# Two-block transformer on one core: in the mixers' second phase, the recurrent branch's steps are put in front of the forgetting-attention step that they are dealt with

## The chip, the cores and the metric

The kernel runs on one core of one Trainium2 chip. The metric is the device time of one execution in microseconds. Engines are named as in the profile: PE (TensorE), DVE (VectorE), ACT (ScalarE), POOL (GpSimd), SP (SyncE).

## The reference, cut to what matters

The program is a first block of two layers and a second block with gated linear attention and a mixture of experts. The change is inside the four mixers of the first block's layers; the rest is the same text in both kernels.

```
for l in range(DEPTH):                                   # DEPTH = 2
    pa, pb, pc, pd = _split(h @ w_in[l], GROUP_COLS)
    ya = _rwkv7_mixer(pa, ...)                           # the recurrent branch
    yb = _diff_attn_mixer(pb, ...)                       # differential attention
    yc = _spatial_gating_mixer(pc, ...)                  # gating
    yd = _forgetting_attn_mixer(pd, ...)                 # forgetting attention
    x = x + g1 * (concatenate([ya, yb, yc, yd]) @ w_out[l])
```

Forgetting attention, for each of 4 heads and each of 4 blocks of 128 queries:

```
s = (einsum('bhqd,bhkd->bhqk', qb, k) * scale + (Fq[..., :, None] - F[..., None, :]))
pr = softmax(where(mask, s, NEG_INF), axis=-1)
out = einsum('bhqk,bhkd->bhqd', pr, v)
```

The recurrent branch is a scan over 512 tokens with a 64 x 64 state per head. The kernel cuts it into chunks of 64 tokens, works out each chunk's inner products and its triangular inverse first, and then scans over the 8 chunks.

## The kernel before, in words

All tensors are fp32, features on the 128 partitions, the 512 tokens along the free dimension. Each layer has three parts: the input projection, `mixers`, and a part with the output projection and the feed-forward network. The weights of the projections pass through a ring of four slots in SBUF.

`mixers` (L1820) runs four streams on each engine: 0 is attention (`attention_stream`: gating, preparation, forgetting attention, then differential attention), 1 is the recurrent branch (`rwkv_stream`), 2 a small modulation stream, 3 the opening of the output projection. Each stream is a generator for each engine, and a `yield` ends a step. `run` (L587) takes a list of stream numbers, the plan, and for each entry lets that stream issue one step on the engine. PE, ACT and DVE get the same plan. It sets the order of the instructions in each engine's queue and nothing else: the streams wait for each other's results by semaphores, an engine executes its queue in order, and so an instruction that waits holds back all that stand behind it. POOL has a short list of its own, and SP issues its DMAs without the plan.

`alternate(first, second)` (L1472) gives `first` zeros with `second` ones spread behind them.

The phase that the change touches deals 17 forgetting steps (stream 0) and 30 recurrent steps (stream 1, second half of the features, `prepare(1)` and `intra(1)`). The names used below:

- **F(u)**, u = 0 to 15, is a step of forgetting attention for unit u, a head and a block of 128 queries. Unit u has (u mod 4) + 1 key blocks of 128, so its tiles are 128 to 512 wide. On PE, F(u) issues the scores of unit u+2 (L778, which wait for the exponentials of unit u), the value sums of unit u-1 (L789), and the transposes of unit u (L806, called **T(u)**), which wait for DVE's scaling of unit u. On DVE, F(u) is the mask and the maximum of unit u+1 (L994, L996), then the reciprocal and the scaling of unit u (L1005, L1008). On ACT it is the exponential of unit u+1 (L898) and the copy of T(u) out of PSUM (L909). F(0) also holds units 0 and 1. F(16) is the last value sum and four tiny DVE operations (L1011 to L1016).
- **p0 to p3** are the four steps of `prepare(1)`. p0: on DVE six operations of 128x512 (L1364 to L1370), on ACT four copies (L1288). p1: on ACT the square (L1291) and three exponentials (L1293 to L1295); on PE transposes (L1143) and the sum of the squares (L1149, which waits for the square); on DVE a clamp of that sum (L1373). p2: on ACT L1298, L1300 and four copies; on DVE L1376 to L1382. p3: on PE one sum (L1153); on DVE L1385 to L1394.
- **m0 to m12** are the 13 micro-steps of `intra(1)`, each in two steps, g0 and g1, for four chunks each. Each has 4, 8 or 12 matmuls or transposes on PE (L1177 to L1212) whose results ACT, DVE or both take. m(k+1) of a group waits for what m(k) of the same group left. m0 starts after L1394 and is followed on DVE by four operations (L1414 to L1417) per group.

A matmul of fp32 operands appears in the trace as two instructions, so "x16" stands for 8 of the code's.

The recurrent steps that `prepare` issues on PE, and its square on ACT, read:

```
eng.wait_ge(s["kk_sq"], of("kk_sq", 1))
eng.matmul(PS(3), c.const("bo64"), ss, start=True, stop=True).then_inc(s["kk_ss"], 1)
...
on(ss, kk, ACT.Square).then_inc(s["kk_sq"], 1)
```

Of the kernel before, what the change touches and what calls it, by code (L numbers as in the profile page):

```python
# [586 lines left out]
def run(engine, streams, plan):  # L587

    programs = [s[engine]() for s in streams]
    for i in plan:  # L590
        next(programs[i])
    for p in programs:
        for _ in p:
            raise ValueError("the plan ends before the stream")
# [877 lines left out]
def alternate(first, second):  # L1472

    plan, done = [], 0
    for i in range(first):
        plan.append(0)
        upto = (i + 1) * second // first
        plan += [1] * (upto - done)
        done = upto
    return plan  # L1480
# [237 lines left out]
def modulation_stream(c, mod, turned_after):  # L1718

    nc = c.nc  # L1720

    def pe():
        for j in range(mod.ada.count):
            mod.sum_quarter(j)
        yield
        nc.tensor.wait_ge(*turned_after)
        mod.turn(nc.tensor)
        yield

    def act():  # L1730
        for j in range(mod.ada.count):
            mod.copy_quarter(nc.scalar, j)
        yield
        yield

    def dve():
        yield
        mod.add_bias(nc.vector)
        yield

    return dict(pe=pe, act=act, dve=dve, sp=lambda: mod.spread(nc.sync), steps=2)
# [78 lines left out]
def mixers(c, sums, w_out, ahead):  # L1820

    nc = c.nc
    mod = ModRows(c, "mod", sums, lambda j: c.vt[:, j // 2, j % 2 * S:(j % 2 + 1) * S], lambda j: c.ps[:, A_BANK + j, :],
                  c.ps[:, A_BANK + 3, :])
    att = attention_stream(c, mod, nc)
    modulation = modulation_stream(c, mod, att["roped"])
    rw = rwkv_stream(c, att, w_out, nc)
    a, b = att["steps"], rw["steps"]
    plan = [1] * b["shift"] + [2] + [0] * a["first"] + [1, 1, 1, 1]
    plan += alternate(a["gating"] + a["prepare"], b["intra"]) + [2]  # L1830
    plan += alternate(a["forget"], b["prepare"] + b["intra"])
    last = alternate(a["diff"], b["scan"])
    at = len(last) - 1 - last[::-1].index(0)
    plan += last[:at] + [3] + last[at:] + [3, 1, 0, 1, 3, 0, 3, 1, 3]
    opened = open_out_stream(c, att, rw, w_out)
    streams = [att, rw, modulation, opened]
    with nc.Block() as block:
        @block.sync
        def _(sp):
            sp.wait_ge(c.tables_in, 32)  # L1840
            att["sp"]()
            modulation["sp"]()
            rw["sp"]()

        @block.gpsimd
        def _(pool):
            c.sweep(pool, [*ahead.loaded, ahead.high, ahead.low])
            run("pool", streams[:2], [0, 1, 0, 1, 0, 1, 0])

        @block.tensor  # L1850
        def _(pe):
            run("pe", streams, plan)

        @block.scalar
        def _(act):
            run("act", streams, plan)

        @block.vector
        def _(dve):
            run("dve", streams, plan)  # L1860
# [379 lines left out]
def block_one_layer(c, layer, ahead, w_out, swept, held):  # L2240
    nc = c.nc
    c.layer = layer
    with c.unswept() as early:
# [3 lines left out]
        with c.stages():  # L2247
            mixers(c, mod_sums, w_out, ahead)
# [1686 lines left out]
```

## Time and profile before

| what | before |
|---|---|
| median of 3 runs | 2516.99 us (2516.23 to 2519.7) |
| the profiled execution, its own time | 2517.74 us |
| its span in the profile | 2516.0 us |
| PE busy | 2267.9 us (90%) |
| DVE busy | 1588.7 us (63%) |
| ACT busy | 1076.0 us (43%) |
| mean granted TensorE clock | 0.967 |
| the changed phase, layer 1 | 269 to 366 us |
| the same phase, layer 2 | 1112 to 1209 us |

How to read it: the times are of one execution, and the span is from the profile's first to its last instruction; 1.7 us of the execution's time lie outside it. The "PEclk" of a stretch is the clock that TensorE was granted as a share of 2.4 GHz: 1.00 is 2.4 GHz and 0.50 is 1.2 GHz; a value between means that it changed in the stretch. A row of the timeline gives the start, the time that the group took, the engine, the line, and in brackets how long the engine sat idle before it and what ended that.

### The profile page before, as it was taken

To read this page: it belongs to the slowest core of one execution; us is meant where nothing else is said; L and a number is where in the kernel's file an instruction comes from. 1 tells how busy PE (TensorE), PEld (TensorE's weight loads), DVE (VectorE), ACT (ScalarE), POOL (GpSimd) and SP (SyncE) were. 2 spreads that over 40 slices of the span, in tenths; PEclk is the share of its full clock that TensorE was granted. 3 is DMA by queue.
4 is the path that set the end of the run, shared out by engine and by line. 5 is a ranking of instruction groups with operands and counts; after the bars stand their busy time and mean duration, and the time that the engine had idled before them with its cause. 6 is when DMAs were issued, how large, how long until landed. Compare 5 with 4: busy or idle time off the path is not lost. (4 is left out here: it accounts for less than half of the span.)

```text
span 2516.0 us, 31937 instructions
## 1 busy us (share of the span) xinstructions
PE 2267.9 (90%) x11349; PEld 1812.1 (72%) x11349; DVE 1588.7 (63%) x2284; ACT 1076.0 (43%) x1628; POOL 123.4 (5%) x201
## 2 busy tenths in 40 slices
PE   4998689899999989877889999999999888799995
PEld 3776566678888877666667888787877676588884
DVE  6655656565557665665665555774543774699996
ACT  3343234443343225342343333413333443588884
POOL 0001110000000000110000000000000000011112
PEclk9999899999999999999999999999999999799997
DMA  7650000222225355200012223354634001699996
GB/s 292 210 184 12 1 34 1 76 84 92 94 79 204 128 166 201 77 1 1 35 43 82 94 92 103 137 172 168 218 109 147 22 1 44 265 410 411 412 412 226
DMA packets 95433, 348.32 MB, mean 138 GB/s; under 512 B 12360, under 2 KB 14520, under 8 KB 95056
## 3 DMA queue, kind: packets, MB, share of 16 engines
q1 hardware_dynamic: 88688, 323.67, 36.1%
q0 software_dynamic: 3888, 14.16, 1.5%
q10 hardware_dynamic: 2736, 8.92, 0.9%
q8 instruction: 71, 1.16, 0.2%
q14 instruction: 50, 0.41, 0.1%
HBM read 333.55 MB, written 21.54 MB: 141 GB/s over the span
## 5 line engine op out<-in xcount | busy, mean ns | idle before, releaser
L500 PE MATMUL ps<-a_hi,w_hi 128*128 128x512 f32 x1344 | 545.1, 406 | 28.5 <-DVE h_lo L406 17.8
L502 PE MATMUL ps<-a_hi,w_lo 128*128 128x512 f32 x1344 | 537.2, 400 | 0.0
L501 PE MATMUL ps<-h_lo,w_hi 128*128 128x512 f32 x1280 | 507.8, 397 | 0.0
L464 DVE TENSOR_TENSOR w_lo<-ring,w_hi 128x1024 fp32r<-128x1024 f32 x178 | 218.1, 1226 | 376.1 <-ACT w_hi L459 375.6
L459 ACT ACTIVATE w_hi<-ring 128x1024 fp32r<-128x1024 f32 x178 | 187.9, 1058 | 510.4 <-PE ps L502 505.0
L500 PEld LDWEIGHTS ps<-a_hi,w_hi 128*128 128x128 f32 x1344 | 255.3, 190 | 98.3 <-issue 26.4
L502 PEld LDWEIGHTS ps<-a_hi,w_lo 128*128 128x128 f32 x1344 | 255.4, 190 | 63.0
L501 PEld LDWEIGHTS ps<-h_lo,w_hi 128*128 128x128 f32 x1280 | 243.1, 190 | 60.8 <-issue 2.9
L3392 DVE TENSOR_TENSOR moe_w_lo<-p,moe_w_hi 128x1024 fp32r<-128x1024 f32 x204 | 240.2, 1219 | 17.8 <-ACT moe_w_hi L3489 12.0
L3489 ACT ACTIVATE moe_w_hi<-p 128x1024 fp32r<-128x1024 f32 x204 | 216.2, 1062 | 68.2 <-PE ps L3432 50.6
L2139 PE MATMUL ps<-p_lo,down_hi 128*128 128x512 f32 x352 | 137.8, 392 | 0.0
L3430 PE MATMUL ps<-moe_w_hi,moe_x_hi 128*128 128x512 f32 x272 | 109.0, 401 | 4.9 <-DVE moe_w_lo L3392 2.9
L3432 PE MATMUL ps<-moe_w_lo,moe_x_hi 128*128 128x512 f32 x272 | 107.5, 395 | 0.0
L3431 PE MATMUL ps<-moe_w_hi,moe_x_lo 128*128 128x512 f32 x272 | 107.3, 395 | 0.0
L2056 ACT ACTIVATE down_hi<-down_raw 128x1408 fp32r<-128x1408 f32 x32 | 44.1, 1379 | 144.7 <-PE ps L2140 144.7
L501 PE MATMUL ps<-y_lo,w_hi 128*128 128x512 f32 x192 | 76.5, 398 | 0.0
L2139 PEld LDWEIGHTS ps<-p_lo,down_hi 128*128 128x128 f32 x352 | 66.1, 188 | 14.4
L291 DVE SCALAR_TENSOR_TENSOR y<-vt,cond,y 128x1024 f32<-128x1024 f32 x56 | 70.7, 1279 | 5.9 <-DMA vt<-in_ada 5.9
L2060 DVE TENSOR_TENSOR down_lo<-down_raw,down_hi 128x1408 fp32r<-128x1408 f32 x32 | 52.0, 1624 | 33.7 <-ACT down_hi L2056 33.4
L1991 DVE SCALAR_TENSOR_TENSOR y<-ps,cols,y 128x510 f32<-128x510 f32 x88 | 65.9, 748 | 11.0 <-DVE y L1988 0.5
L1961 ACT ACTIVATE y<-ps,cols 128x512 f32<-128x512 f32 x88 | 67.2, 764 | 9.4 <-PE ps L502 9.4
L1988 DVE SCALAR_TENSOR_TENSOR y<-ps,cols,y 128x511 f32<-128x511 f32 x88 | 65.6, 745 | 4.6 <-ACT y L1961 4.6
(645 smaller groups left out, 4196.0 us busy)
## 6 DMA issues: line engine op xcount, KB each, us to landing
ring<-in_ffn_up SPq DMA_DIRECT2D x88, 512.0 KB, 3.4
ring<-in_w_in SPq DMA_DIRECT2D x72, 512.0 KB, 5.2
p<-in_moe_gate SPq DMA_DIRECT2D x68, 512.0 KB, 7.1
p<-in_moe_up SPq DMA_DIRECT2D x68, 512.0 KB, 6.8
p<-in_moe_down SPq DMA_DIRECT2D x68, 512.0 KB, 8.4
vt<-in_ada SPq DMA_DIRECT2D x64, 512.0 KB, 4.0
p<-in_ada SPq DMA_DIRECT2D x48, 512.0 KB, 5.5
down_raw<-in_ffn_down SPq DMA_DIRECT2D x32, 704.0 KB, 5.2
```

Of the source, the lines that this page charges most:

```text
L291: ins = nc.vector.scalar_tensor_tensor(out, self.piece[b], factor, out, ALU.mult, ALU.add)
L459: self.c.nc.scalar.activation(self.c.w_hi[:, s % 2, :], self.c.slot(s), ACT.Copy).then_inc(self.high, 1)
L464: self.c.nc.vector.tensor_tensor(self.c.w_lo[:, s % 2, :], self.c.slot(s), self.c.w_hi[:, s % 2, :].bitcast(F32), ALU.subtract).then_inc(s ...
L500: nc.tensor.matmul(bank, c.w_hi[:, s % 2, at], hi(kt), start=(kt == self.order[0]), stop=False)
L501: nc.tensor.matmul(bank, c.w_hi[:, s % 2, at], lo(kt), start=False, stop=False)
L502: return nc.tensor.matmul(bank, c.w_lo[:, s % 2, at], hi(kt), start=False, stop=(kt == self.order[-1]))
L2139: nc.tensor.matmul(bank, down.w_hi[n % 2][:, at], c.p_lo[:, kt, :], start=False, stop=False)
L3392: ops.tensor_tensor(m.w_lo[:, n % 4, :], m.raw[n], m.w_hi[:, n % 4, :].bitcast(F32), ALU.subtract).then_inc(low[n], 1)
L3430: nc.tensor.matmul(bank, x[0], w_hi, start=start, stop=False)
L3431: nc.tensor.matmul(bank, x[1], w_hi, start=False, stop=False)
L3432: return nc.tensor.matmul(bank, x[0], w_lo, start=False, stop=stop)
L3489: nc.scalar.activation(m.w_hi[:, n % 4, :], m.raw[n], ACT.Copy).then_inc(high[n], 1)
```

## The change

One line of `mixers`. Before, each forgetting step is followed by its one or two recurrent steps; now F(0) comes first, and each of the other 16 forgetting steps follows its one or two recurrent steps.

```diff
@@ -1828,7 +1828,7 @@
     a, b = att["steps"], rw["steps"]
     plan = [1] * b["shift"] + [2] + [0] * a["first"] + [1, 1, 1, 1]
     plan += alternate(a["gating"] + a["prepare"], b["intra"]) + [2]
-    plan += alternate(a["forget"], b["prepare"] + b["intra"])
+    plan += [0] + [1 - i for i in alternate(b["prepare"] + b["intra"], a["forget"] - 1)]
     last = alternate(a["diff"], b["scan"])
     at = len(last) - 1 - last[::-1].index(0)
     plan += last[:at] + [3] + last[at:] + [3, 1, 0, 1, 3, 0, 3, 1, 3]
```

The two plans of the phase, 47 entries each:

```
before 01011011011010110110110101101101101011011011011
after  01101101101101101101101011011011011011011011010
```

The recurrent steps that stand ahead of F(0), F(1), ... F(16):

```
before  0 1 3 5 7  8 10 12 14 15 17 19 21 22 24 26 28
after   0 2 4 6 8 10 12 14 15 17 19 21 23 25 27 29 30
```

No instruction is added or removed, and the queues of POOL and SP are the same.

ACT, the start of the phase, from p0's copies (L1288) on. Before:

```order
L1288 ACTIVATE p<-p 64x4x64 x4
L898 ACTIVATE ring,small<-ps,small 128x384
L909 ACTIVATE ring<-ps 128x256
L1291 ACTIVATE ring<-ring 128x512
L1293 ACTIVATE vt<-ring 128x512
L1294 ACTIVATE ring<-ring 128x512
L1295 ACTIVATE ring<-ring 128x512
L1298 ACTIVATE ring<-ring 128x512
```

and after:

```order
L1288 ACTIVATE p<-p 64x4x64 x4
L1291 ACTIVATE ring<-ring 128x512
L1293 ACTIVATE vt<-ring 128x512
L1294 ACTIVATE ring<-ring 128x512
L1295 ACTIVATE ring<-ring 128x512
L898 ACTIVATE ring,small<-ps,small 128x384
L909 ACTIVATE ring<-ps 128x256
L1298 ACTIVATE ring<-ring 128x512
```

The square and the exponentials of p1 no longer stand behind the exponential of F(1) and the copy of T(1).

PE, the same place, from T(0) on. Before:

```order
L806 MATMUL ps<-k,ring 128x128
L778 MATMUL ps<-w2b,vt 128x512
L789 MATMUL ps<-ring,vt 64x128
L806 MATMUL ps<-k,ring 128x128 x2
L1143 MATMUL ps<-k,p 128x128 x8
L1149 MATMUL ps<-ring,k 128x512
L778 MATMUL ps<-ring,vt 128x128
L789 MATMUL ps<-ring,vt 64x128 x2
L806 MATMUL ps<-k,ring 128x128 x3
L1153 MATMUL ps<-p,k 128x512
L1177 MATMUL ps<-h,p 128x128
```

and after:

```order
L806 MATMUL ps<-k,ring 128x128
L1143 MATMUL ps<-k,p 128x128 x8
L1149 MATMUL ps<-ring,k 128x512
L778 MATMUL ps<-w2b,vt 128x512
L789 MATMUL ps<-ring,vt 64x128
L806 MATMUL ps<-k,ring 128x128 x2
L1153 MATMUL ps<-p,k 128x512
L778 MATMUL ps<-ring,vt 128x128
L789 MATMUL ps<-ring,vt 64x128 x2
L806 MATMUL ps<-k,ring 128x128 x3
L1177 MATMUL ps<-h,p 128x128
```

The transposes and the sum of p1 stand ahead of F(1), and p3's sum ahead of F(2), which is now the last thing before m0.

DVE, around the end of p3 and m0. Before:

```order
L1391 TENSOR_TENSOR h<-ring 64x8x64 x2
L1394 TENSOR_TENSOR p<-ps,p 128x512
L1414 TENSOR_TENSOR ring<-ps,k 128x512
L1415 TENSOR_TENSOR ring<-ps,k 128x512
L1416 TENSOR_TENSOR y<-ring,k 128x512
L1417 TENSOR_TENSOR ring<-ps,k 128x512
L994 TENSOR_TENSOR ps<-ps,k 128x128
L996 TENSOR_REDUCE small<-ps 128x1
L1005 RECIPROCAL small<-small 128x1
L1008 TENSOR_SCALAR ring<-ring,small 128x512
```

and after:

```order
L1391 TENSOR_TENSOR h<-ring 64x8x64 x2
L1394 TENSOR_TENSOR p<-ps,p 128x512
L994 TENSOR_TENSOR ps<-ps,k 128x128
L996 TENSOR_REDUCE small<-ps 128x1
L1005 RECIPROCAL small<-small 128x1
L1008 TENSOR_SCALAR ring<-ring,small 128x384
L1414 TENSOR_TENSOR ring<-ps,k 128x512
L1415 TENSOR_TENSOR ring<-ps,k 128x512
L1416 TENSOR_TENSOR y<-ring,k 128x512
L1417 TENSOR_TENSOR ring<-ps,k 128x512
```

F(2) now stands between p3 and m0; behind it both groups of m0 come ahead of F(3), where before only the first did.

## Rows read from the trace of the kernel before

**Rows 1.** Windows, core 0: stretch and length, each engine's busy us, PEclk, DMA share, GB/s

```profile
269.00:294.00 25.00, 11.84 (x42) 6.88 (x41) 19.06 (x35) 10.59 (x26) 6.00 (x9) 0.71 0.00 1
...
1113.50:1138.00 24.50, 11.35 (x38) 6.84 (x38) 18.21 (x33) 10.00 (x25) 5.27 (x8) 0.68 0.00 1
```

**Rows 2.** Waits of PE, 269 to 366 us: us in total, times, longest

```profile
PE ps L806 <- DVE ring L1008: 22.6, 15, 4.5
```

**Rows 3.** Timeline of DVE, p0 to p3: start, us, line, tiles, idle before

```profile
277.90 0.30 DVE L994 TENSOR_TENSOR ps<-ps,k 128x128 f32<-128x128 f32 x1
...
283.21 0.69 DVE L1373 TENSOR_SCALAR ring<-ps 128x512 f32<-128x512 f32 x1 [3.96 <-PE ps L1149]
...
286.83 0.30 DVE L994 TENSOR_TENSOR ps<-ps,k 128x128 f32<-128x128 f32 x1
...
287.96 0.42 DVE L1008 TENSOR_SCALAR ring<-ring,small 128x384 f32<-128x384 f32 x1
288.30 0.68 DVE L1385 TENSOR_TENSOR ring<-ring 128x512 f32<-128x512 f32 x1
...
292.62 0.69 DVE L1394 TENSOR_TENSOR p<-ps,p 128x512 f32<-128x512 f32 x1
```

**Rows 4.** Timeline of ACT, p0's copies and p1's square

```profile
274.04 1.72 ACT L1288 ACTIVATE p<-p 64x256 f32<-64x256 f32 x4
...
280.31 0.62 ACT L1291 ACTIVATE ring<-ring 128x512 f32<-128x512 f32 x1
```

**Rows 5.** Timeline of PE, from T(1) to T(3)

```profile
279.31 0.69 PE L806 MATMUL ps<-k,ring 128*128 128x128 f32 x2 [4.26 <-DVE ring L1008]
279.79 1.91 PE L1143 MATMUL ps<-k,p 128*128 128x128 f32 x8
281.49 1.68 PE L1149 MATMUL ps<-ring,k 128*128 128x512 f32 x2
...
288.44 0.90 PE L806 MATMUL ps<-k,ring 128*128 128x128 f32 x3 [4.46 <-DVE ring L1008]
289.13 1.92 PE L1153 MATMUL ps<-p,k 128*128 128x512 f32 x2
293.46 0.77 PE L1177 MATMUL ps<-h,p 128*128 128x128 f32 x2 [2.42 <-DVE p L1394]
...
301.41 0.66 PE L806 MATMUL ps<-k,ring 128*128 128x128 f32 x4 [3.27 <-DVE ring L1008]
```

**Rows 6.** Timelines of PE and DVE, m0 of the first half, no F between

```profile
212.34 6.48 PE L1177 MATMUL ps<-h 128*128 128x128 f32 x32 [4.46 <-DVE p L1394]
...
216.19 0.69 DVE L1414 TENSOR_TENSOR ring<-ps,k 128x512 f32<-128x512 f32 x1 [3.99 <-PE ps L1177]
...
218.97 0.68 DVE L1414 TENSOR_TENSOR ring<-ps,k 128x512 f32<-128x512 f32 x1
```

**Rows 7.** Windows, short stretches: columns as in rows 1

```profile
212.00:215.00 3.00, 2.66 (x12) 2.69 (x13) 0.20 (x1) 0.00 (x0) 0.00 (x0) 0.50 0.00 0
...
286.00:288.00 2.00, 0.00 (x0) 0.00 (x0) 1.86 (x6) 0.86 (x3) 0.00 (x0) 0.55 0.00 0
...
296.00:298.00 2.00, 2.00 (x14) 1.57 (x13) 0.63 (x1) 0.00 (x0) 0.00 (x0) 0.89 0.00 0
298.00:300.00 2.00, 0.14 (x2) 0.00 (x0) 1.90 (x4) 0.00 (x0) 0.00 (x0) 1.00 0.02 4
```

**Rows 8.** Timeline of PE: T(5), both groups of m2, T(6), T(15)

```profile
315.17 0.44 PE L806 MATMUL ps<-k,ring 128*128 128x128 f32 x2 [1.73 <-DVE ring L1008]
315.44 3.74 PE L1177 MATMUL ps<-ring 128*128 128x128 f32 x32
...
321.41 0.55 PE L806 MATMUL ps<-k,ring 128*128 128x128 f32 x3 [1.43 <-DVE ring L1008]
...
360.33 0.66 PE L806 MATMUL ps<-k,ring 128*128 128x128 f32 x4 [0.58 <-DVE ring L1008]
```

**Rows 9.** Timeline of DVE: the first maximum of differential attention

```profile
366.33 0.29 DVE L1026 TENSOR_TENSOR ps<-ps,k 128x128 f32<-128x128 f32 x1
```

## The prediction, made before the changed kernel was run

> **What bounds the phase now.** I first read the busy time by stretch: in the 25 us at the phase's start PE is busy for 11.84 us and DVE for 19.06, at a granted clock of 0.71, and the same stretch of layer 2 reads alike, 11.35 and 18.21 us at 0.68 [rows 1]. So everything below counts twice. Then the waits of PE: of its idle time in the phase nearly all, 22.6 us in 15 waits, stands in front of the transposes T(u), each released by DVE's scaling L1008 [rows 2]. Neither engine is saturated; the bound is the chain that passes between them: recurrent matmuls on PE, DVE's operations on them, DVE's part of F, T(u), the next matmuls. The timelines show where this chain itself stops. DVE is free at 279.2, but p1's clamp L1373 starts at 283.21 after 3.96 us of idleness [rows 3], because it needs L1149, L1149 needs the square L1291, and ACT had that square behind F(1) until 280.31, though its queue was free from 275.76 on, when L1288 ended [rows 4]. PE's own transposes L1143 stood behind T(1), at 279.79 [rows 5]. This stop the change removes.
>
> **The change, part by part.** All durations are of the profiled execution of 2517.74 us (span 2516.0), 0.75 above the median of the runs shown; since the change is a difference I take it off the median, 2516.99.
>
> *Start, up to m0.* The square now runs at about 275.8. PE does the second half of L1143 (0.85 of its 1.70 us until L1149), then L1149, whose result DVE took 1.72 us after its start (281.49 to 283.21) [rows 3, 5]: L1373 can start at 275.85 + 0.85 + 1.72 = 278.4. These are prices at the low clock; at the high one L1373 starts when p0 leaves DVE, 277.9 [rows 3]. From there DVE has no wait: p1 and p2 take 3.62 (283.21 to 286.83), F(1) about 1.3 (1.41 from L994 to T(1)), p3 4.32 up to L1394 and 0.6 for it, F(2) 1.61 from L994 to T(2), and T(2) holds PE 0.69 [rows 3, 5]. 278.4 + 3.62 + 1.3 + 4.32 + 0.6 + 1.61 = 289.85 for T(2), 290.5 for m0, which started at 293.46. **Gain at this point 2.9 us** (3.4 with the high clock), with the same work done. What is late next is p3's DVE work and F(2), which are now in front of m0 and covered by nothing.
>
> *m0 and F(3).* Both groups of m0 now come ahead of F(3). The first half of the branch shows this order undisturbed: 3.85 us from PE's start to L1414 (212.34 to 216.19) and 2.78 for each group on DVE (216.19 to 218.97) [rows 6]. F(3) adds 1.26, by adding up as for F(2), with a narrower maximum. T(3) comes at 290.5 + 3.85 + 5.56 + 1.26 = 301.2, against 301.41 [rows 5], but with one recurrent step more behind it. The lead has become that step.
>
> *F(4) to F(16).* I add each slot up as: T(u) (0.17 to 0.50 by width), the recurrent matmuls (both groups of m2 3.57, from 315.44 to the next matmul; 8 groups of the code's half of that, by count), 0.2 until DVE has them, 0.6 per DVE copy or add of 512, and 1.2 to 1.6 for F. For T(5) to T(6) it gives 0.27 + 3.57 + 0.2 + 0.61 + 1.59 = 6.24, which is what the rows have (315.17 to 321.41) [rows 8]. With the new slots (m1 both 8.5; m2 6.2; m3 6.2; m4 4.2; m5g0 4.3; then pairs across the groups 5.1, 3.6, 4.7, 5.05, 4.5, 4.5, 3.7) T(15) comes 60.5 us after T(3), at 361.7; before, it was at 360.33 [rows 8]. The pairs across the groups cost most: m9, m10 and m11 each had a slot of their own in which only ACT or only two adjacent adds had to be awaited, and one of those slots, with scores, value sums and matmuls of two kinds, is now bound by PE. Behind T(15) only m12g1 and the last value sum are left: 1.4 us of matmuls, 0.2, the copy 0.6 and four tiny operations 0.65 put differential attention's first maximum at 364.55, against 366.33 [rows 9]. **1.8 us per layer stay of the 2.9**, 3.6 in all (4.6 with the high clock at the start). Everything behind waits for this work, so it moves along.
>
> *Queues of SP and POOL.* No DMA is moved. POOL's copies wait for scores that come within half a microsecond of where they were. Cost nil; uncovered, one collision with DVE's scaling would cost some 0.3 us.
>
> *The clock.* Its price no row of before shows at the new place, so it is bounded. PE was granted 1.2 GHz when m0 began and 2.4 GHz again between 296 and 298 (0.89) [rows 7]. Then PE paused 3.27 us in front of T(3) and kept 2.4 GHz (1.00 in 298 to 300) [rows 5, 7]. Pauses of 4.46 us lost it, the one up to 288.44 (0.55 in 286 to 288) and the one up to 212.34 [rows 5, 6, 7]. In the new order PE has m0's second group done early and waits for 5.56 us of DVE work: its pause is 301.2 less some 296.7 to 298.2, 3.0 to 4.5 us, between the two cases seen. If the clock is lost there, m1, which is on the chain, starts at 1.2 GHz. Recovery took some 3 us after 293.46 [rows 5, 7]; behind 212.34 it took nearly the whole of m0, since 32 trace matmuls took 6.48 us there (0.50 in 212 to 215) against 3.74 for m2's 32 [rows 6, 7, 8]. So 1.4 to 2.8 us per layer are lost. Lower end 0 (kept), upper end 2.8; I take 1.0 per layer, as lost in one of the two layers, since the new pause lies between the row that kept it and the rows that did not.
>
> The Trainium skill, "TensorE: Matmul & The Clock Gate", section "HAM oscillation", says that bursts of matmuls with longer pauses between them are throttled again in every pause. The trace agrees for 286 to 288 and disagrees for the pause before T(3) [rows 7]. By the skill's rule the gain would be given back in both layers.
>
> Sum: 2516.99 - 3.6 + 2.0 = **2515.4 us**.
>
> **The rivals.**
> 1. *The clock holds in both layers.* For it: it held in the pause of 3.27 us. Against: the new pause is probably longer. 2516.99 - 3.6 = 2513.4; with the high clock at the start too 2512.4. Chance 0.25.
> 2. *The start's lead is kept whole.* If the pairs across the groups cost no more than the aligned ones, 2.9 per layer stay: 2511.2. Against: DVE then has to take two results per slot, and the sum of slots says otherwise. Chance 0.13.
> 3. *Lost in both layers* (what the skill's page would have): 3.6 less 2 x 2.0 gives back everything, 2517.4. Chance 0.15.
> 4. *Slower.* The clock stays low through the whole of m1 and its slot in both layers. m1 is 24 matmuls of the code against m2's 16, by count 5.3 us at 2.4 GHz [rows 8], and twice that at 1.2. Net 5.3 - 1.8 = 3.5 per layer, 2524.0. It decides once the low clock costs the 1.8 won and another 2.5, that is after some 9 us at 1.2 GHz behind T(3), longer than either recovery seen. Chance 0.10.
>
> My forecast has 0.37.
>
> **How the numbers follow.** About 0.2% (5 us) is what a measurement of this kernel can tell from no change. Faster than that is rival 2 and the edge of rival 1: 0.13 + 0.05 = 0.18. Slower is rival 4 and 0.02 of mishap: 0.12. The rest, 0.70, lies within. The range reaches from rival 2 with a little over (2510.8) to 2520.5, which leaves out most of rival 4; the forecast's own is 2514 to 2517.
>
> **What would show it.** Right: L1373 within 1 us behind p0 with no wait of 4 us; m0 2.5 to 3.5 us earlier after the phase's start; T(3) unchanged within half a microsecond; T(15) later by 1 to 2; the first L1026 earlier by 1 to 2.5; a granted clock below 1 for 3 to 6 us behind T(3) in one layer. Wrong: T(3) itself 2 us early (my price for both groups of m0 is too high), L1026 3 us early (slots priced too high), or a low clock elsewhere in the phase.

## The result, and the profile of the changed kernel

The changed kernel takes 2531.75 us (median of 5 runs, 2529.91 to 2532.17) against 2519.64 us for the kernel before in its runs beside it (median of 5, 2516.23 to 2519.7): a ratio of 1.0047, 95% interval [1.0036, 1.0057]. It is slower by 12 us. The prediction was 2515.4 in a range of 2510.8 to 2520.5; rival 4 (slower through a low clock in m1, 2524.0) named the mechanism, and even that was too small. Of the distance to the forecast 2.65 us are the base: the prediction started from 2516.99, the median of three runs of the kernel before, and the five runs beside the kernel after have 2519.64.

| what | before | after |
|---|---|---|
| profiled execution, its own time | 2517.74 us | 2530.51 us |
| its span | 2516.0 us | 2528.8 us |
| mean granted TensorE clock | 0.967 | 0.961 |
| first L1026 after the start of the phase, layer 1 and layer 2 | 96.14, 96.18 us | 100.93, 100.92 us |
| T(3) after the start of the phase, both layers | 31.22, 31.25 us | 31.86, 31.84 us |
| T(4) after T(3), both layers | 7.79, 7.79 us | 13.64, 13.36 us |

The start of the phase is here the first operation of the layer's mixers on DVE behind the preparation (270.19 us before, 270.04 us after; 1113.26 and 1119.66 us in layer 2). It serves to lay phases of different kernels over each other.

The page's first part shows that PE is busy for 20 us more (2267.9 before), with the same 11349 instructions:

```profile
PE 2287.6 (90%) x11349; PEld 1828.1 (72%) x11349; DVE 1589.1 (63%) x2284; ACT 1076.0 (43%) x1628; POOL 124.4 (5%) x201
```

**The start.** The timeline of DVE over p0 to p3, F(2), m1 and the end of the phase (compare [rows 3, 9]):

```profile
278.59 0.69 DVE L1373 TENSOR_SCALAR ring<-ps 128x512 f32<-128x512 f32 x1 [1.59 <-PE ps L1149]
...
281.17 1.04 DVE L1377 SCALAR_TENSOR_TENSOR p<-p,cols,ring 128x512 f32<-128x512 f32 x1
282.25 0.47 DVE L1378 COPY small<-vt 128x8 f32<-128x8 f32 x1
...
288.39 0.69 DVE L1394 TENSOR_TENSOR p<-ps,p 128x512 f32<-128x512 f32 x1
...
307.24 0.69 DVE L1419 TENSOR_TENSOR p<-ps,k 128x512 f32<-128x512 f32 x1 [5.40 <-PE ps L1185]
...
370.97 0.30 DVE L1026 TENSOR_TENSOR ps<-ps,k 128x128 f32<-128x128 f32 x1 [0.29 <-PE ps L819]
```

The wait of 3.96 us in front of L1373 [rows 3] is 1.59 us. But two operations of p2 are longer than in the kernel before, whose timeline has

```profile
284.53 0.75 DVE L1377 SCALAR_TENSOR_TENSOR p<-p,cols,ring 128x512 f32<-128x512 f32 x1
285.32 0.17 DVE L1378 COPY small<-vt 128x8 f32<-128x8 f32 x1
```

and the timeline of POOL says what they now lie beside: POOL's two copies, which start 5 us later than before (281.06 against 275.97). After:

```profile
279.75 0.52 POOL L699 MEMSET vt<- 1x512 f32 x1 [6.54 <-PE ps L778]
...
281.06 0.60 POOL L676 COPY w2b<-p 64x512 f32<-64x512 f32 x1
281.73 0.96 POOL L676 COPY vt<-p 64x512 f32<-64x512 f32 x1
```

POOL had waited for the scores L778 of F(1), and these stand on PE behind L1149 now (278.28 against 273.66). In the kernel before the copies lay beside p0's last two operations and stretched those:

```profile
275.94 0.92 DVE L1369 TENSOR_SCALAR ring<-ring,cols 128x512 f32<-128x512 f32 x1
276.89 0.98 DVE L1370 SCALAR_TENSOR_TENSOR ring<-ring,p 128x512 f32<-128x512 f32 x1
```

They take 0.48 and 0.69 us in the kernel after. But DVE now waits for L1149 behind them, so that saving is hidden, while the stretch of L1377 and L1378 is on the chain.

**The loss.** The timeline of PE from p1's sum to T(4) (compare [rows 5]):

```profile
276.57 1.91 PE L1149 MATMUL ps<-ring,k 128*128 128x512 f32 x2
...
290.73 0.90 PE L806 MATMUL ps<-k,ring 128*128 128x128 f32 x3 [4.41 <-DVE ring L1008]
291.42 0.64 PE L1177 MATMUL ps<-h,p 128*128 128x128 f32 x2
...
297.71 0.87 PE L789 MATMUL ps<-ring,vt 128*64 128x128 f32 x6
301.90 0.66 PE L806 MATMUL ps<-k,ring 128*128 128x128 f32 x4 [3.32 <-DVE ring L1008]
302.39 0.39 PE L1177 MATMUL ps<-p,h 128*128 128x128 f32 x2
302.62 0.33 PE L1184 MATMUL ps<-p,h 128*128 128x64 f32 x2
...
303.69 0.53 PE L1184 MATMUL ps<-p,h 128*128 128x64 f32 x2
...
312.12 1.59 PE L778 MATMUL ps<-ring,vt 128*128 128x384 f32 x2
313.64 1.97 PE L789 MATMUL ps<-ring,vt 128*64 128x128 f32 x8
315.54 0.48 PE L806 MATMUL ps<-k,ring 128*128 128x128 f32 x1
```

m0 starts at 291.42 (293.46 before), T(3) at 301.90 (301.41 before), as forecast with one more recurrent step done. From the second L1184 on, the same instruction takes 0.53 us where the first took 0.33, and m1 runs from 302.39 to 312.12 without a gap. The kernel before has T(4) at

```profile
309.20 0.33 PE L806 MATMUL ps<-k,ring 128*128 128x128 f32 x1 [1.00 <-DVE ring L1008]
```

The windows give the granted clock (columns as in rows 1):

```profile
300.00:302.00 2.00, 0.10 (x1) 0.10 (x2) 1.75 (x5) 0.46 (x2) 0.00 (x0) 1.00 0.00 0
302.00:304.00 2.00, 2.00 (x14) 2.00 (x15) 0.00 (x0) 0.60 (x1) 0.00 (x0) 0.71 0.00 0
...
314.00:316.00 2.00, 2.00 (x10) 1.67 (x9) 0.78 (x3) 0.56 (x2) 0.00 (x0) 0.50 0.00 0
316.00:318.00 2.00, 2.00 (x18) 2.00 (x17) 0.00 (x0) 0.28 (x1) 0.00 (x0) 0.88 0.00 0
...
1158.00:1160.00 2.00, 2.00 (x12) 2.00 (x11) 0.00 (x0) 0.00 (x0) 0.00 (x0) 0.50 0.00 0
```

```profile
304.00:314.00 10.00, 10.00 (x44) 8.92 (x44) 2.97 (x5) 0.00 (x0) 0.00 (x0) 0.50 0.01 2
```

The clock is at 2.4 GHz when the pause in front of T(3) ends, falls about a microsecond after PE has resumed, and stays at 1.2 GHz for some 13.6 us; in the row of 304 to 314 PE is busy for 10.00 of 10.00 us. It rises only behind T(4), in m2. In layer 2 it is low for as long, from 1152.8 to 1166.4. The kernel before has 1.00 in the same two microseconds, in which it runs m0's second group:

```profile
302.00:304.00 2.00, 2.00 (x21) 2.00 (x19) 0.10 (x1) 0.60 (x1) 0.00 (x0) 1.00 0.00 0
```

PE's wait for L1008 in the phase is now 18.8 us in 14 waits where it was 22.6 in 15 [rows 2]: T(4) has no idle time in front of it any more, PE itself is late.

```profile
PE ps L806 <- DVE ring L1008: 18.8, 14, 4.4
```

The two phases account for 9.5 of the 12.8 us between the profiled executions (2 x 4.8). The first L1026 of the phase and the last one of differential attention are 65.8 and 66.2 us apart where it was 64.7 in both layers before: another 2.6 us. There too the clock fell: four matmuls L819 (128x384) took 2.85 us, 1.57 before, at these rows of after and of before:

```profile
375.23 2.85 PE L819 MATMUL ps<-p,vt 128*128 128x384 f32 x4
```

```profile
370.39 1.57 PE L819 MATMUL ps<-p,vt 128*128 128x384 f32 x4
```

The stretches from there to the next stage (L1961, see experiment 6) add 1.1 us (86.9 and 86.8 for 86.6 and 86.0), and 0.4 us less are spent elsewhere.

### The profile page after: what moved, and what is told of

It is laid out like the page before. It is cut to its first block and busy times, and to the rows that moved or that the text cites. A ratio compares the mean times of both kernels' runs of the same rounds, so it can differ in the third digit from the quotient of the medians.

```text
span 2528.8 us, 31937 instructions
## 1 busy us (share of the span) xinstructions
PE 2287.6 (90%) x11349; PEld 1828.1 (72%) x11349; DVE 1589.1 (63%) x2284; ACT 1076.0 (43%) x1628; POOL 124.4 (5%) x201
## 3 DMA queue, kind: packets, MB, share of 16 engines
q10 hardware_dynamic: 2736, 8.92, 0.9%
## 5 line engine op out<-in xcount | busy, mean ns | idle before, releaser
L1961 ACT ACTIVATE y<-ps,cols 128x512 f32<-128x512 f32 x88 | 67.2, 764 | 9.4 <-PE ps L502 9.4
```

## Experiments

All were timed against the kernel before on the same chip. "Ahead" is the table of recurrent steps that stand ahead of F(0), F(1), ..., as in the section on the change. "Wide matmuls" are 128x128 by 128x512 products of two constants into a PSUM bank that is free there and is overwritten afterwards; they change no result. Added lines shift those below them: L810, L849, L1012 and L1047 of the kernels with wide matmuls are L806, L845, L1008 and L1043 of the kernel before. Where the text says that T(3), T(4) or the first L1026 "comes at" a time, it is counted from the start of the phase.

### 1. Hold PE busy in the pause in front of T(3)

```diff
+            if u == 3:
+                eng.wait_ge(fx["copied"], u)
+                for _ in range(3):
+                    eng.matmul(PS(2), c.const("ident"), c.const("cos"), start=True, stop=True)
             eng.wait_ge(fx["scaled"], u + 1)
```

> The changed kernel with three added matmuls (ident times cos, 128x512) in front of T(3), in the pause in which PE waited 3.32 us. They write the bank that T(3) overwrites and change no result. Clock theory (the changed kernel loses because TensorE is granted 1.2 GHz from just behind T(3) until m2 is under way, 13.6 us from T(3) to T(4) where 8.5 were expected): the clock stays at 1.00 through m1, T(4) comes 8.5 to 8.8 us after T(3), each layer gets 5 us faster, and the time falls from 2531.8 to about 2521.5. Order theory (the slots of the new order cost the time, whatever the clock): no gain, or a loss of up to 1 us per layer for the added matmuls, 2531 to 2533.

Measured: 2522.69 us, ratio to before 1.0019 [1.0009, 1.0029]; the kernel after had 1.0047. In the timeline of PE the three fill the pause, and the window over m1 reads 1.00:

```profile
297.53 2.84 PE L805 MATMUL ps<-k 128*128 128x512 f32 x6
300.86 0.66 PE L810 MATMUL ps<-k,ring 128*128 128x128 f32 x4 [0.49 <-DVE ring L1012]
```

```profile
302.00:306.00 4.00, 4.00 (x39) 4.00 (x37) 1.38 (x2) 0.15 (x1) 0.00 (x0) 1.00 0.02 4
```

T(3) is where it was (31.86 after the start of the phase) and T(4) follows after 8.53 us instead of 13.64. The first L1026 comes at 95.39 and 95.34, 5.54 and 5.58 us earlier than in the kernel after and 0.75 and 0.84 earlier than before. So the low clock behind T(3) costs 5.5 us per layer, and without it the order is slightly ahead of the old one. The time as a whole stays above before: in layer 2 this kernel lost the clock again behind differential attention (90.2 us for that stretch where layer 1 has 86.9; see experiment 6).

### 2. The control: the same three matmuls in the kernel before

> The kernel before with the same three added matmuls in front of T(3), as a control. Its clock is 1.00 there already. Clock theory: the matmuls fit in the pause of 3.27 us and nothing changes, within 1 us of the kernel before. If the matmuls themselves cost time (they hold T(3) back), it is 0.2 to 1 us per layer slower, and e1 has to be read with that.

Measured: 2519.93 us, ratio 1.0002 [0.9993, 1.0012]; first L1026 at 96.09 and 96.29 (96.14 and 96.18 before). The matmuls themselves cost and bring nothing where the clock is held anyway.

### 3. The new start alone

```diff
-    plan += [0] + [1 - i for i in alternate(b["prepare"] + b["intra"], a["forget"] - 1)]
+    ahead_of = (0, 2, 4, 5, 7, 8, 10, 12, 14, 15, 17, 19, 21, 22, 24, 26, 28)
+    for i, n in enumerate(ahead_of):
+        plan += [1] * (n - (ahead_of[i - 1] if i else 0)) + [0]
+    plan += [1] * (b["prepare"] + b["intra"] - ahead_of[-1])
```

Ahead of F(0) to F(2) as after, from F(3) on as before.

> The kernel before with the new order up to m0 only: recurrent steps ahead of F(0) to F(16) are 0 2 4 5 7 8 10 and so on, from F(3) on as before. Clock theory: m0 starts about 1.9 us earlier per layer as in the changed kernel's trace, both groups of m0 stand apart as before, T(3) is 1.9 us earlier and the lead stays to the end, if the clock holds in front of m0's second group as it did before: 2 x 1.9 off the kernel before, about 2514 to 2516. If it is lost there, which is possible since the pause stays at 3.3 us but lies elsewhere, the second group and m1 run at 1.2 GHz and it is slower than before by up to 10 us. Order theory: the gain of 1.9 per layer in any case.

Measured: 2519.06 us, ratio 0.9995 [0.9985, 1.0006]. T(3) comes at 29.41, 1.8 us earlier than before. T(4) follows after 9.33 us (7.79 before), with a granted clock of 0.50 in 298 to 300, and the first L1026 comes at 95.88 and 95.55: only 0.3 and 0.6 us of the lead are left. The start's gain stands in the trace; a short low clock takes most of it, and the time as a whole does not differ from before by more than the noise. The forecast of 2514 to 2516 was missed, and the order theory, a gain of 1.9 us in any case, does not hold either.

### 4. The old start with the rest of the new order

Ahead of: 0 1 3 6 8 10 12 14 15 17 19 21 23 25 27 29 30.

> The kernel before with the new order from m0 on only: recurrent steps ahead of F(0) to F(16) are 0 1 3 6 8 10 12 14 15 17 19 21 23 25 27 29 30. Clock theory: T(3) comes about 2 us later than in the changed kernel, the clock is lost behind it as there, and the loss is the changed kernel's plus the start's gain that is missing, 2 x 1.9: about 2535. If the clock is kept here, 2523 to 2526. Order theory: 2535 with the clock at 1.00 all through m1 is not possible; it expects the slots behind T(4) to be longer than the changed kernel's sum, and they are not.

Measured: 2533.18 us, ratio 1.0054 [1.0035, 1.0072]. T(3) comes at 33.76, 1.9 us later than in the kernel after: the start's gain seen from the other side. T(4) follows 14.47 us later, and the granted clock is 0.50 for the whole stretch 306 to 316. So the loss does not need the new start: it comes with m1 right behind T(3).

### 5. What brings the clock back: m0's second group behind T(3), or wide matmuls inside m1

The first of the two kernels puts m0's second group between T(3) and m1 (ahead of: 0 2 4 5 8 10 12 14 15 17 19 21 23 25 27 29 30):

> The change's order, but with only m0's first group ahead of F(3); the second group and both groups of m1 follow T(3) (recurrent steps ahead: 0 2 4 5 8 10 12 14 ..., so one slot differs). Theory A, what follows the pause decides: wide matmuls of m0 (128x128) behind T(3) hold or quickly restore the clock, and m1 runs at 2.4 GHz: PEclk 1.00 in m1, T(3) at some 29.4 and T(4) some 12 us behind it (two groups of m1, one of m0 with its DVE work), L1026 at 95 to 96 behind the anchor. Theory B, any pause of over 3 us in this place puts m1 at the low clock: T(4) some 16 us behind T(3), L1026 at 100 or later and a time as the kernel after.

Measured: 2522.99 us, ratio 1.001 [1.0, 1.002]. The clock is lost in the pause and back within m0, and m1 runs at 2.4 GHz:

```profile
297.60 1.12 PE L806 MATMUL ps<-k,ring 128*128 128x128 f32 x4 [2.58 <-DVE ring L1008]
...
309.95 0.33 PE L806 MATMUL ps<-k,ring 128*128 128x128 f32 x1 [0.85 <-DVE ring L1008]
```

```profile
298.00:300.00 2.00, 2.00 (x11) 2.00 (x10) 0.00 (x0) 0.60 (x1) 0.00 (x0) 0.50 0.00 0
300.00:302.00 2.00, 2.00 (x17) 2.00 (x16) 0.43 (x1) 0.00 (x0) 0.00 (x0) 0.81 0.00 0
302.00:308.00 6.00, 5.67 (x46) 5.00 (x45) 4.20 (x7) 0.00 (x0) 0.00 (x0) 1.00 0.01 3
```

The first L1026 comes at 96.67 and 96.49 (forecast 95 to 96), against 100.9 in the kernel after. The pause (2.58 us) was shorter than the 3.32 us of the kernel after and lost the clock all the same; what differs is what follows it.

The second is the kernel after with three wide matmuls between m1's groups:

```diff
+                    if q == 1 and m == 1 and g == 0:
+                        eng.wait_ge(att["fx"]["copied"], 4)
+                        for _ in range(3):
+                            eng.matmul(c.ps[:, A_BANK + 2, :], c.const("ident"), c.const("cos"), start=True, stop=True)
```

> The kernel after, with three wide matmuls (128x128 by 128x512) between m1's two groups, where PE was granted 1.2 GHz while it was busy throughout. Theory A, the narrow matmuls of m1 keep the clock low and wide ones bring it back: the granted clock reads 1.00 during or right behind the three, m1's second group takes some 2.5 us instead of some 4.9, and T(4) follows T(3) by 13 to 15 us, the three themselves (2.8 to 5 us) eating what they give. Theory B, only the time since the pause counts, not what PE does: the clock rises no earlier behind T(3) than in the kernel after (some 16 us), so the three cost 5 us at the low clock and T(4) comes some 17 to 18 us behind T(3); the time is some 6 to 8 us above the kernel after.

Measured: 2532.36 us, ratio 1.0045 [1.0029, 1.006], the same as the kernel after. The timeline of PE (the three, then m1's second group) and the windows:

```profile
305.88 3.62 PE L1217 MATMUL ps<-k 128*128 128x512 f32 x6
309.34 0.38 PE L1177 MATMUL ps<-p,h 128*128 128x128 f32 x2
309.56 0.33 PE L1184 MATMUL ps<-p,h 128*128 128x64 f32 x2
```

```profile
304.00:306.00 2.00, 2.00 (x12) 2.00 (x11) 0.00 (x0) 0.00 (x0) 0.00 (x0) 0.50 0.00 0
306.00:308.00 2.00, 2.00 (x4) 0.85 (x4) 1.38 (x2) 0.00 (x0) 0.00 (x0) 0.62 0.00 0
308.00:310.00 2.00, 2.00 (x11) 1.23 (x9) 0.00 (x0) 0.00 (x0) 0.00 (x0) 1.00 0.00 0
```

The clock rises within the three, some 7 us behind T(3) (8 in layer 2) instead of some 15, and m1's second group takes 2.6 us (309.34 to 311.96) instead of 5.1 (307.00 to 312.12). T(4) follows T(3) by 14.39 us (13.64 in the kernel after): what they cost, they nearly give back. That is theory A, and theory B (only time counts) would have had T(4) at 17 to 18. Two streams of matmuls that fill PE alike thus do not bring the clock back alike.

### 6. The clock taken out, and a better kernel

Three wide matmuls in front of T(2) and of T(3) each (`if u in (2, 3)`), once in the change's order and once in that of experiment 3:

> The kernel after with three wide matmuls in front of T(2) and T(3), so that m0 and m1 both run at 2.4 GHz: what the new order is worth with the clock taken out. Theory that the clock is all of the loss: m0 1 to 1.6 us shorter than with the matmuls in front of T(3) alone, where L1026 came 95.4 us behind the anchor, so L1026 at 94.0 to 94.6 and a time 2 to 4 us below before. Rival, m0 is bound by DVE at either clock: L1026 at 95.4 as there, time as before.

> Another order (recurrent steps ahead of F(0), F(1), ...: 0 2 4 5 7 8 10 12 14 15 17 19 21 22 24 26 28, so the new order up to F(2) and the old one from F(3) on), with three wide matmuls into a free bank in front of T(2) and of T(3). Clock theory: the start's lead stays (T(3) some 29 us behind the phase's anchor at 31.2 before), m0 runs at 2.4 GHz and gives 1 to 1.6 us more, no dip behind T(3): first L1026 some 93 to 94 us behind the anchor against 96.1 before and 100.9 after; time 4 to 6 us below before, unless a low clock elsewhere takes it. Rival, the order itself costs what was lost: L1026 at 96 or later and a time within 2 us of before.

| | T(3) | T(4) | first L1026, layer 1 and 2 | time | ratio to before |
|---|---|---|---|---|---|
| before | 31.22 | 39.01 | 96.14, 96.18 | 2519.79 us | |
| change's order, held | 29.85 | 38.38 | 93.38, 93.39 | 2525.64 us | 1.0019 [1.001, 1.0028] |
| order of experiment 3, held | 27.10 | 34.89 | 92.03, 92.00 | 2512.81 us | 0.9975 [0.9964, 0.9985] |

In the phase both did what the clock theory asks, and more (m0 at 2.4 GHz as well). But the change's order, 2.8 us ahead per layer when the phase ended, came out 0.2% slower in time. The loss lies behind differential attention: from its last L1026 to the next stage's first L1961 it took 92.5 and 92.6 us (86.6 and 86.0 before, 86.9 twice in the other kernel). The profiled execution of 2529.0 us was the longest of the kernel's eleven (the shortest took 2519.56), so the trace may show more of this loss than a median run has. The place is the pause in front of the last L849, differential attention's last transposes. Windows of this kernel, and of the other at the same work:

```profile
432.50:435.50 3.00, 2.76 (x13) 2.64 (x14) 0.19 (x1) 0.83 (x3) 0.00 (x0) 0.55 0.00 0
435.50:438.50 3.00, 3.00 (x21) 2.55 (x21) 0.00 (x0) 3.00 (x6) 0.00 (x0) 0.50 0.00 0
...
446.00:447.00 1.00, 1.00 (x3) 0.53 (x2) 0.59 (x1) 0.69 (x1) 0.00 (x0) 0.78 0.00 0
```

```profile
430.00:433.00 3.00, 2.77 (x30) 2.64 (x31) 0.17 (x1) 1.95 (x6) 0.00 (x0) 1.00 0.00 0
433.00:436.00 3.00, 3.00 (x37) 2.63 (x37) 1.11 (x6) 3.00 (x6) 0.00 (x0) 1.00 0.00 0
```

and the pause itself in the timelines of PE, first of the kernel that lost the clock, then of the one that kept it:

```profile
432.74 1.11 PE L849 MATMUL ps<-k,ring 128*128 128x128 f32 x4 [1.39 <-DVE ring L1047]
```

```profile
430.23 0.66 PE L849 MATMUL ps<-k,ring 128*128 128x128 f32 x4 [1.39 <-DVE ring L1047]
```

The same pause of 1.39 us with the same instructions before and behind it, and in the first the clock stays low until 446.4, for nearly 14 us. To test it, one wide matmul was put there in both kernels, and in the kernel before:

```diff
+            if u == NU - 1:
+                eng.wait_ge(df["copied"], u)
+                eng.matmul(PS(2), c.const("ident"), c.const("cos"), start=True, stop=True)
             eng.wait_ge(df["mixed"], u + 1)
```

> The kernel of the run before that held the clock through m0 and m1 (three wide matmuls in front of T(2) and T(3)) and then lost it for some 12 us behind differential attention's last pause of 1.39 us, in both layers, with one wide matmul (under 1 us) put into that pause. Theory, the low clock there was all that ate the lead: L1026 at 93.4 behind the anchor as before, the stretch from the last L1026 to the gate of the next stage (L1961) at 86.9 us instead of 92.5, and a time of 2513 to 2516, 4 to 7 below before. Rival, the order of the change costs something behind the phase that is not the clock: the stretch stays at over 90 at a granted clock of 1.00, time 2523 or more.

Measured: 2516.49 us, ratio 0.9979 [0.9969, 0.9989], where the same kernel without it had 1.0019. The stretch behind took 87.6 and 86.7 us. **With the clock held in these places the change's order is 0.2% faster than the kernel before**, which has none of the added matmuls. That is not the worth of the order alone: of the 2.8 us per layer, 2.0 came with the three matmuls in front of T(2) (95.39 to 93.38), which let m0 run at 2.4 GHz, and the old order was not run with those. The comparison of orders with the same three matmuls in front of T(3) is experiment 1 against experiment 2, 95.39 against 96.09 and 95.34 against 96.29: 0.7 to 1.0 us per layer. The lead was not the whole 2.8 us in layer 2, where a low clock between T(2) and T(3) put T(3) at 30.94.

> The fastest kernel so far (new start, old order from F(3) on, three wide matmuls in front of T(2) and T(3)) with the same one wide matmul in differential attention's last pause. Its profiled run kept the clock there, so its trace changes little: L1026 at 92.0 behind the anchor, the stretch behind at 86.9 in both layers. Theory, its timed runs lose the clock there sometimes: median 1 to 3 us below 2512.8 and a narrower spread. Rival, the pause is kept anyway: the same median within 1 us.

Measured: 2511.99 us (2510.57 to 2512.41), ratio 0.9961 [0.9947, 0.9975]: the fastest of all, 0.4% below before. The first L1026 comes at 92.01 and 92.06. Against 2512.81 without the added matmul (2510.15 to 2515.84) the median is no more than 0.8 us lower, within the rival's bound, and the intervals of the two ratios overlap; the spread is narrower, in six runs against eight.

> The kernel before with the same one wide matmul in differential attention's last pause, and nothing else. Theory, the spread of before's own runs (2514 to 2528) is a clock lost behind that pause in some executions: spread halved, median 1 to 3 us below before. Rival, its spread comes from elsewhere: median within 1 us of before, spread as before; the added matmul itself costs nothing, as it ends in the pause.

Measured: 2521.0 us (2518.08 to 2522.85, 12 runs), ratio 1.0001 [0.9993, 1.001]; before had 2516.36 to 2529.94 in 23 runs beside it. The median is as the rival has it. None of the 12 runs is long, but only two of before's 23 were above 2524 us, so their absence can be chance: that a lost clock at this place makes the longest runs of before is not shown. It does not set the median.

## Why the prediction was wrong, step by step

- **The clock: the step that failed.** The pause was foreseen ("between the two cases seen"; 3.32 us in front of T(3)), and so was it that m1 would run at 1.2 GHz if the clock was lost there. What failed was the price, "1.4 to 2.8 us per layer are lost ... I take 1.0". It was taken from how long the low clock had lasted in m0, "some 3 us" and "nearly the whole of m0", which are matmuls 128 wide, and it was counted for one of the two layers. Behind T(3) it lasted 13.6 us, in both layers, and cost 5.54 and 5.58 us per layer (kernel after against experiment 1). Of the 5.1 us in the slot, m1 took 4.4 (9.73 us against 5.31 with the clock held) and the scores and value sums behind it 0.7; another 0.4 fell into m2. The upper bound of 2.8 was no bound, since the row it came from was of another kind of matmul. Rival 4 had that mechanism with 5.3 us and a chance of 0.10; it deserved the weight of an end of the range.
- **The rule of the skill.** The Trainium skill, "TensorE: Matmul & The Clock Gate", section "HAM oscillation", describes bursts of matmuls that are shorter than the pause behind them, so that the next burst starts throttled. The trace of the kernel after agrees where that is the case: in layer 2 the pause of 4.46 us in front of T(2) stands behind a burst of 3.5 us (1132.38 to 1135.87), and the granted clock is 1.00 in 1136 to 1137 and 0.50 in 1141 to 1145. In front of T(3) it is not the case, neither before (4.7 us of matmuls from 293.46 on, pause 3.27) nor after (7.9 us from 290.73 on, pause 3.32). So the prediction was wrong to say that the trace disagrees there, and that the gain would go back in both layers does not follow from that section; that it did go back is no support for it. Rival 3, built on it, had 2517.4.
- **The start, mis-sized.** Forecast: 2.9 us per layer, measured 1.9 to 2.0 (m0 at 291.42 for 293.46; T(3) 1.9 later in experiment 4). L1373 came at 278.59 (forecast 278.4). Of the rest 0.6 us lie in L1377 and L1378 beside POOL's copies, 0.2 in L1373 and 0.1 in L1394. The sentence "POOL's copies wait for scores that come within half a microsecond of where they were" was wrong: they waited for L778 of F(1), and that was moved behind L1149, by 4.6 us. The queue was looked at, the instruction that it waits for was not.
- **m0 and F(3), right.** 10.48 us from m0 to T(3) (forecast 10.67).
- **The slots, right once the clock is held.** T(3) to T(4) took 8.53 us in experiment 1 (forecast 8.5); T(4) to the first L1026 55.00 in experiment 1 and 55.43 in the kernel after (forecast 54.85). Also the statement that the aligned groups are cheaper: with three wide matmuls in front of T(2) and T(3) in both, the old pairing from F(3) on is 1.35 us per layer ahead (92.03 against 93.38).
- **What stayed per layer without the clock.** Forecast 1.8 us, measured 0.75 and 0.84 (experiment 1); the 1.0 lacking is the start's.
- **"Everything behind waits for this work, so it moves along."** It does, but not only in time: what lies behind met low clocks at other places. That cost 2.6 us in differential attention of the kernel after, and 12.5 behind it in the profiled execution of the first kernel of experiment 6 (92.5 - 86.6 and 92.6 - 86.0). No term stood for it.

What stays open: why a pause of a given length loses the clock in one kernel and not in another. The kernel before has a pause of 3.27 us in front of T(3) [rows 5] and kept the clock, the kernel after 3.32 and lost it, and 3.17 in layer 2, where it lost it too; two pauses of 1.39 us with the same work around them differ as well, and so do the two layers of experiment 1's kernel behind theirs of 1.38 us. The experiments show that the low clock is the loss and what ends it, not what decides that it comes. It was not tried apart either whether the width of m1's matmuls or the weight loads between them (8.92 of 10.00 us in the row of 304 to 314, 0.85 of 2.00 beside the wide ones) keeps it low.

## What to carry to other kernels

When an order is changed, ask of each pause of TensorE what follows it, and price a low clock by the matmuls that would run under it: with m0's 128x128 ones the clock was back at 2.4 GHz in 3 to 6 us, with the added 128x512 ones in 2 to 3, while m1's mix with 128x64 right behind such a loss ran at 1.2 GHz to its end. A few wide matmuls on constants in such pauses, ended before the awaited result comes, cost nothing that could be measured in the kernel before (1.0002 and 1.0001) and brought the changed order from a ratio of 1.0047 to 0.9979. And of a queue that is "not touched", look up which moved instruction its next entry waits for.

## What the runs showed of the hardware that was not expected

- PE ran at 1.2 GHz for some 13.6 us while it was busy without a gap (10.00 of 10.00 us in 304 to 314), in both layers; m1's matmuls took 5.31 us with the clock held and 9.73 without.
- A pause of 1.39 us was followed by nearly 14 us at 1.2 GHz in one kernel and by none in another, at identical work: 92.5 against 86.9 us for the stretch.
- DVE operations stretched beside POOL's copies: L1377 1.04 us for 0.75 and a copy of 128x8 0.47 for 0.17. When the copies moved, the stretch moved with them, from L1369 and L1370 (0.92 and 0.98 us, 0.48 and 0.69 without).
